# Adding the expert rows of four token tiles with accumulating transfers from GpSimd's queue

## The reference, cut to what matters

```python
x = x + gt1 * out                       # after the mixer; the kernel calls it x2
h = rmsnorm(x, p['g_norm_ffn'][l]) * (1.0 + sc2) + sh2
x = x + gt2 * hier_moe(h, l, p)         # two expert rows for each token, weighted and summed
...
y = rmsnorm(x, p['g_final'])            # y_prompt, y_sample
```

## Time and profile before

| | us |
|---|---|
| median of 3 runs (1388.09 to 1389.97) | 1389.63 |
| the profiled execution's own time | 1394.4 |
| its span, first to last instruction | 1392.7 |
| PE busy | 1333.9 (96%) |
| DVE busy | 614.5 (44%) |
| ACT busy | 324.1 (23%) |
| POOL busy | 128.6 (9%) |
| mean granted TensorE clock | 0.985 |

### The profile page before, as it was taken

The page is one execution under the profiler, slowest core; times in us unless marked ns, Lnnn a source line. Parts: engine busy times, 40 slices in busy tenths (PEclk is TensorE's granted clock), DMA queues, the critical chain, the costliest instruction groups (busy, mean ns, idle before and its releaser), DMA issues. The chain is left out here.

```text
span 1392.7 us, 21248 instructions
## 1 busy us (share of the span) xinstructions
PE 1333.9 (96%) x8719; PEld 795.1 (57%) x8719; DVE 614.5 (44%) x1304; ACT 324.1 (23%) x692; POOL 128.6 (9%) x157
## 2 busy tenths in 40 slices
PE   4899999999999999999999999999999999999997
PEld 3344448876667666666567666788873433333333
DVE  6743352325343145870392234343675532222258
ACT  4200002545544210122322122111221111101113
POOL 0000001024000042010000000000001111111110
PEclk9999999999999999999999999999989999999999
DMA  9424323329002362422412174530057899999775
GB/s 365 130 91 155 125 91 131 124 70 346 23 18 72 82 213 79 149 69 75 86 62 96 47 248 141 183 128 31 31 197 266 345 415 405 411 404 408 311 294 235
DMA packets 123987, 248.98 MB, mean 179 GB/s; under 512 B 24331, under 2 KB 88475, under 8 KB 114649
## 3 DMA queue, kind: packets, MB, share of 16 engines
q1 hardware_dynamic: 100768, 200.34, 40.2%
q0 software_dynamic: 11600, 30.54, 5.9%
q10 hardware_dynamic: 11522, 16.73, 3.4%
HBM read 208.30 MB, written 46.24 MB: 183 GB/s over the span
## 5 line engine op out<-in xcount | busy, mean ns | idle before, releaser
L2440 PE MATMUL psum<-ring,big 128*128 128x256 f32 x512 | 116.7, 386 | 0.0
L1317 PE MATMUL psum<-h_t,ring 128*128 128x352 f32 x368 | 111.4, 461 | 1.1 <-ACT gate_units L1608 1.1
L2589 PE MATMUL psum<-w_gate_up,u_rows 128*32 128x512 f32 x608 | 107.8, 597 | 2.3 <-ACT u_rows L2756 1.4
L2440 PEld LDWEIGHTS psum<-ring,big 128*128 128x128 f32 x512 | 97.9, 194 | 13.7 <-issue 0.4
L2589 PE MATMUL psum<-ring,u_rows 128*32 128x512 f32 x576 | 99.1, 594 | 0.7 <-ACT u_rows L2756 0.7
L1317 PEld LDWEIGHTS psum<-h_t,ring 128*128 128x128 f32 x368 | 69.0, 190 | 38.3 <-issue 1.6
L2612 PE MATMUL psum<-big 128*32 128x512 f32 x736 | 86.3, 610 | 0.0
L474 PE MATMUL psum<-big,u_rows 128*128 128x512 f32 x144 | 63.9, 593 | 0.0
L2109 PE MATMUL psum<-big,h_t 128*128 128x352 f32 x192 | 60.5, 459 | 1.9 <-PEq L2062 1.9
L2766 ACT ACTIVATE big<-psum 128x256 f32<-128x256 f32 x23 | 8.8, 383 | 226.9 <-PE psum L2589 226.9
L2589 PE MATMUL psum<-big,u_rows 128*32 128x512 f32 x288 | 58.2, 613 | 1.8 <-DMA w_gate_up<-in_w_exp_up 1.8
(11 more groups left out here) (560 smaller groups left out, 2175.0 us busy)
## 6 DMA issues: line engine op xcount, KB each, us to landing
big<-in_w_exp_down SPq DMA_DIRECT2D x32, 1024.0 KB, 10.5
ring<-in_w_ada SPq DMA_DIRECT2D x24, 1024.0 KB, 7.8
w_gate_up<-in_w_exp_gate SPq DMA_DIRECT2D x13, 1024.0 KB
w_gate_up<-in_w_exp_up SPq DMA_DIRECT2D x13, 1024.0 KB
ring<-in_w_exp_gate SPq DMA_DIRECT2D x13, 1024.0 KB, 5.2
ring<-in_w_exp_up SPq DMA_DIRECT2D x13, 1024.0 KB, 8.0
ring<-in_w_in SPq DMA_DIRECT2D x11, 1024.0 KB, 10.1
h_t<-tmp_gates SPq DMA_DIRECT2D x48, 176.0 KB, 2.6
```

The source lines that it names most:

```text
L1317: m = T_.matmul(bank[4 + u % 4][:, 0:CW], w_[:, k, c0:c0 + P], ht3[:, k, j * CW:(j + 1) * CW], start=(k == 0), stop=(k == KT - 1))
L2440: m = T_.matmul(bank[2 * (i % 2) + b // 2][0:r, (b % 2) * WB:(b % 2 + 1) * WB], merged_t[:, k, t * P:t * P + r], w[:, k, :], start=(k == 0 ...
L2589: m = T_.matmul(bank[i][at, :], x_t[i][:, k * P + CHUNK * c:k * P + CHUNK * (c + 1)], w_gu[use_of(e, GSLOTS)[0]][:, :, k, :], start=(k == ...
```

## The change

Tiles 3, 5, 6 and 7 leave the two groups and form a third, `BY_DMA`. SP loads no expert rows for them. Instead GpSimd, once all scatters have landed, issues one accumulating transfer for each of the four tiles, from the first half of `expert_rows` in HBM onto `x2` in SBUF; then, for each tile, it waits until that one has landed and issues the second, from the other half. Only then does it come to the loop and its `loop_block`. VectorE's `add_loop` waits for the second transfer of a tile before it adds the PSUM pair. VectorE's `add_rows` for tiles 3 and 5 and TensorE's four identity products for tiles 6 and 7 are gone. No other line is changed.

```diff
-        BY_VECTOR, BY_PRODUCT = (0, 1, 3, 5), (2, 4, 6, 7)
+        BY_VECTOR, BY_PRODUCT, BY_DMA = (0, 1), (2, 4), (3, 5, 6, 7)
...
-                    for t in [TT] + [t for t in ADD_ORDER if t != TT]:
+                    for t in [TT] + [t for t in ADD_ORDER if t != TT and t not in BY_DMA]:
...
                 for b in range(ROUNDS - 3, ROUNDS):
                     scatter(b)
+                for i in range(2):
+                    pool.wait_ge(s_yst[i], 16 * ((ROUNDS + 1 - i) // 2))
+                for t in BY_DMA:
+                    G.dma_start(x2[:, t, :], scratch["expert_rows"][t * P:(t + 1) * P, :], accum_op=ALU.add).then_inc(s_fa[t], 16)
+                for t in BY_DMA:
+                    pool.wait_ge(s_fa[t], 16)
+                    G.dma_start(x2[:, t, :], scratch["expert_rows"][TOKENS + t * P:TOKENS + (t + 1) * P, :], accum_op=ALU.add).then_inc(s_fb[t], 16)
                 with pool.Fori(0, turns) as n:
                     loop_block(n + 1, bass.ds(n + 1, 1))
...
                         dve.wait_ge(s_lrp, NT * n + a + 1)
+                        if t in BY_DMA:
+                            dve.wait_ge(s_fb[t], 16)
```

## The result

The changed kernel takes 1394.82 us (median of 10 runs, 1390.73 to 1398.14) against 1390.12 us for the kernel before on the same chip: a ratio of 1.0031, 95% interval 1.0017 to 1.0046. Timed once more, at the end of the study, it was 1396.03 against 1390.45 us, 1.0041 (1.0028 to 1.0055). One of the ten runs of before took 1480.83 us and is left out of the ratio. By the two ratios the changed kernel is slower by 0.3 to 0.4%, 4.3 to 5.7 us.

A forecast was written before the change was run, and what follows sets the result against it. In the tail TensorE, VectorE and, for the first 25 us, the loads run close together. Slowed loads nearly cancel the 4.1 us saved: tile 4 +0.9 to +2.6, taken as +1.5 on 1389.63, gives 1391.1 us; range 1385.8 to 1400.5.

The forecast's parts named there:

- the faster case: Tail: loads hardly hurt by accumulating transfers, 3.1 to 4.1 us gained, 1385.5 to 1386.5; chance 30%.
- r = 3: Far bound, slower case: an accumulating row takes three times a plain row's DMA time; tile 4 9.9 us late, 1399.5; 22%.
- the forecast: Tail: doubled row cost and equal queue turns nearly cancel the gain; +1.5 us, 1391.1, own range 1389.5 to 1393.5; 42%.
- What is removed, 4.1 us: Tail: VectorE's additions and TensorE's identity products go; tile 4 is added 4.1 us earlier if transfers cost nothing.
- r = 2: DMA engines: an accumulating row takes twice a plain row's time; plain loads beside it keep 137 GB/s.
- Equal turns, row by row: DMA engines alternate between GpSimd's and SP's queues, one row each; each queue near 137 GB/s.
- The start of the accumulating transfers, 4 us after S: Their data begins moving at about 1348, 4 us after the last scatter landed and GpSimd's wait ended (1343.99).
- tile 0's first rows, which I called safe: Their load is through by 1348, before accumulating data moves, so VectorE's start at 1349.07 stays.
- a sign to look for: If GpSimd's queue starts well before 1348, the first loads suffer too: slower by one or two us.
- up to 1.7 us of lower clock at tile 4: TensorE, after waiting gaps: tile 4's last four matmuls at 1.2 GHz take 1.7 us more.
- The wait for the second transfers: VectorE, before adding the PSUM pair: second transfers land by 1367.2 to 1378.7, each before its tile's turn; no cost.
- `loop_block` and its gather: GpSimd, queued behind the fourth first-half transfer: gather lands late but is needed only after tile 7; costs nothing.

The follow-up runs named there:

- e1: Changed kernel without its eight accumulating transfers and VectorE's waits for them, output left incomplete: 1385.91 us against 1389.93 for the kernel before.
- e4: Changed kernel with GpSimd issuing the accumulating transfers only when tile 2's second rows have landed: ratio 1.0041 to the kernel before.
- e2: Changed kernel with its eight GpSimd transfers as plain copies into unused buffers, nothing added: ratio 1.0003 to the kernel before.
- e11: Changed kernel, unedited, profiled and timed once more: 1396.03 us against 1390.45 for the kernel before, ratio 1.0041.
- e5: Changed kernel with GpSimd issuing the accumulating transfers only when tile 0's second rows have landed: ratio 1.0017 to the kernel before.
- e7: Changed kernel with only tiles 3, 5 and 7 by accumulating transfers, reordered, started after tile 0's second rows: ratio 1.0009 to the kernel before.
- e8: Changed kernel, all four tiles, started after tile 0's second rows, tile 3's transfers ahead of tile 6's and 7's: ratio 1.0032 to the kernel before.
- e6: Changed kernel with only tiles 5 and 7 by accumulating transfers, started after tile 3's second rows: ratio 0.9989 to the kernel before.
- e12: The version with only tiles 5 and 7 by accumulating transfers, started after tile 3's second rows, timed again: ratio 0.9973 to the kernel before.
- e3: Changed kernel with only the first four accumulating transfers, the four tiles' second expert rows left out: ratio 1.0033 to the kernel before.
- e9: Kernel before, unedited, profiled and timed a second time: ratio 1.0007 against itself.
- e10: Kernel before, unedited, profiled a third time: one run, no ratio, tail of 46.9 us after the last scatter landed.

## Why the prediction was right or wrong

The measured time lies in the stated range. That says little by itself: the range of 14.7 us reaches from the faster case to r = 3. More telling is that the mechanism of the forecast is the one at work, with its r and its turns. The size is not as forecast: I gave 1.5 us (the forecast's own range ends at 1393.5), and 4.3 to 5.7 were measured. Slower by more than 0.2% had a chance of 36%, no change to be told 39%.

- **What is removed, 4.1 us: right.** e1 has 4.6 us at tile 4's addition (26.2 against 30.8), and 4.0 us in the medians, whose interval is wide.
- **r = 2: right.** 69.3 against 36.3% for the same bytes, 207 GB/s alone (e4), 206 GB/s for q1 when only the addition is taken away (e2). The Trainium skill, "Collectives: The Full Stack", in its section on why ReduceScatter is half of AllGather, puts an add in flight at half the speed of a copy, because of two source reads. The traces agree on the speed, for a transfer from HBM onto SBUF (207 against 412 GB/s); the two reads themselves no row shows.
- **Equal turns, row by row: right once both queues are busy.** 905 packets against 907; q1 at 136 GB/s where 137 was worked out. It does not hold for the first microsecond in e2 (71 against 15).
- **The start of the accumulating transfers, 4 us after S: the term that was mis-sized.** Loads are slowed from about S + 2 us on: by S + 4 q1 has moved 0.51 MB instead of 0.84, and 0.33 MB at 137 GB/s are 2.4 us. So tile 0's first rows, which I called safe, are awaited for 5.67 us, and its second addition starts at S + 11.8 instead of 8.6. Every landing after that stays as late, 3.2 us in the first profile and 2.1 in e11: tile 1's second rows (19.4 and 18.4 against 16.3), tile 4's second (34.8 and 33.7 against 31.6). The prediction had named this as a sign to look for, at a price of one or two us.
- **Why 4 us was wrong.** I took it from the stores of zeros and from the tail's gather. It is not that these are another kind of transfer: issued while SP's loads fill the engines, the accumulating ones take just as long to appear, 4 us or more in e5, e7 and e8 and 3 to 4 in e6 and e12. Issued beside SP's first loads (changed, e11, e3), they slow q1 within 2 us, and in e4, where the loads are nearly through, q0's first packets come 1.5 to 2 us after the issue. Both rows that I used had a busy q1 beside them; at S it was only filling up. What it is in the queues that makes the difference was not tested.
- **The clock: a second term, in the baseline.** I charged up to 1.7 us of lower clock at tile 4 of the changed kernel. It fell at the first products after `ly`, and there it costs next to nothing: VectorE waits 0.22 us for these products, and TensorE then waits 1.3 us for tile 2's rows all the same. In the first profile of before the same drop is on the path (VectorE waits 0.85 and 0.91 us for TensorE), and e9 and e10 don't have it: 32.4 against 30.8 and 30.7. The forecast was laid out from that profile and put on the median, so it was some 1.6 us too low against executions without the drop.
- **Together.** Tile 4's addition is 4.9 us (e11) to 6.0 us (first profile) later than in e9. 0.9 of it was forecast, 1.6 is the baseline's clock, 2.1 to 3.2 the early start, and 0.3 the last four matmuls, 2.0 us where I had 1.7.
- **The wait for the second transfers: hidden, as forecast.** VectorE never waits for `s_fb` in the changed kernel, because all else is late. In e4, e5, e7 and e8, where the loads are nearly on time, that wait is the next limit.
- **`loop_block` and its gather: nothing**, as forecast.

What stays open: why the landings are 3.2 us late in one profile of the changed kernel and 2.1 in the other, where 2.4 was worked out. How often the kernel before has the drop of its clock can't be told from three profiles. S itself moves by up to 10 us between executions. The mean granted clock from 420 to 1080 us is 0.97 in e4, whose S is the latest, and 0.99 in e11 and e12, whose S is the earliest, which fits; it was not looked into further.

## What to carry to other kernels

Work that is moved from a busy engine to a transfer is not free where the DMA engines are already full: an accumulating row takes the time of two, and equal turns mean that the loads which everybody waits for pay for it. Before moving work there, lay the landings of the existing loads against the moments at which they are needed, and start the new transfers after the last load that has no slack; the same idea on two tiles, started 14 us later, gained 0.1 to 0.3% (with no change inside one of its two intervals) where on four it lost 0.3 to 0.4%. Take a delay from a row whose queues are in the same state, or carry both ends through the sum: the same transfers were felt within 2 us or after 4, by what stood in the other queue. And lay out a forecast from more than one profile of the kernel before, for a drop of the clock in one of them may be missing in the next.

## What the runs showed of the hardware

- An accumulating transfer from HBM onto SBUF writes 207 GB/s alone and 137 GB/s beside a full queue of plain loads, which then get 137 as well; plain copies on the same queue leave 206 and take 206.
- GpSimd's issue of an accumulating 512 KB transfer takes 0.85 us against 0.53 to 0.59 for a plain one (e2), and the first four took 3.65 us together.
- Accumulating transfers slowed the loads within 2 us of their issue when SP's queue had just begun, and showed no packet for 4 us when it was full (e5, 1.54 MB of loads in these 4 us); a gather beside full loads took as long.
- TensorE's first products after a stretch with little work ran at the lower clock (granted 0.50 to 0.57 in stretches of 4 us) in both profiles of the changed kernel, in e2 and in one of three profiles of the kernel before. In that one TensorE was busy for 1.93 of the 3 us ahead, and 16 matmuls took 9.14 us; in e9, without the drop, it was 2.28 us, and 7.45.
- The drop counts only where TensorE is on the path: 2.7 us in e2 and 1.6 in the first profile of before, 0.2 in the changed kernel, where the loads were later still.
